# A hybrid decoder step on one core: the input projection from rows laid out turned, with the norm's vector in the weights and the token shift finished by DMA

## The chip, the core and the metric

The kernel runs on one core of a Trainium2 chip: TensorE (PE; its weight loads are shown apart, as PEld), VectorE (DVE), ScalarE (ACT), GpSimd (POOL), and SyncE (SP), which here only issues transfers. The metric is device microseconds for one execution of the whole program, median of several runs. Lower is better.

## What is computed

One inference step of a one-layer decoder over 1024 prompt rows and 64 sample rows (8 sequences of 8), which share all weights. The program is a chain of stages with a barrier between them: projection, mixers (retention and RWKV-7), attention over memory tokens, routing, experts, combination. The change touches the first two:

```python
P = rmsnorm(x, g_mix) @ w_in                  # 1024 -> 3328 columns
ret_p, rw_p = P[..., :1536], P[..., 1536:]    # retention | RWKV
prev = concatenate([s_shift[:, None, :], rw_p[:, :-1]], axis=1)
rw_s = rw_p + (prev - rw_p) * rwkv_mu         # token shift, 1792 columns
s_shift_new = rw_p[:, -1]                     # an output
r, kr, vr, hw, ha, hg = split(rw_s, ...)      # into the RWKV recurrence
```

For the prompt the row before the first is zero; for a sample sequence it is its row of `state_shift`.

## The kernel before

Rows stand in nine tiles of 128: tiles 0 to 7 are the prompt, tile 8 (`NT`) holds the 64 sample rows and 64 rows of padding. Every f32 product is made of three fp32r products: x_hi·w_hi + x_hi·w_lo + x_lo·w_hi, where `hi` is a rounded copy made by ACT and `lo` the remainder made by DVE.

`phase_project` runs over 8 chunks of 416 columns (`NCH`, `W`), and in each over the 9 tiles. Per tile PE makes 8 (`KC`) x 3 matmuls of 128x416: 24 x 9 x 8 = 1728. Ahead of a tile's first use its rows are loaded (`pj_x`), ACT squares and scales them by 1/rms (`norm`, L238 and L240), POOL takes the power (L232), PE turns them (`turn`, L286, 8 transposes), and DVE multiplies by `g_mix` and splits them (L214 to L216). The weights are split a chunk at a time (ACT L254, DVE L199). ACT copies a finished bank out (L247) and stores it to the DRAM array `proj` (L249), one row further down, so that row 0 can be the zero row. PE runs chunks 1 to 6 in a loop of instructions.

`phase_mixers` loads tile j of `proj` (`mx_pin`, 13 KB a row), the RWKV columns of the row above (`mx_prev`) and the rotary table (`mx_rope`), in `load(j)` on SP. DVE does the token shift, three operations over three column ranges: `shift_v` (768 columns), `shift_k` and `shift_r` (512 each), all at L467 to L469. In `pair(i)` these are set between the steps of tile i's triangular inverse: `level(i, l)` is five rounds in which PE makes products with `TTT`, DVE masks them into `X` (L571), PE multiplies again, and ACT copies `TTT` (L854). Tile i+1's preparation is interleaved with it on every engine: POOL's rotation into `mx_qk` (L718 to L723), which PE turns between levels 1 and 2 (L962), ACT's `lora_act` (L783 to L785), which waits for `shift_v`. `load(i + 2)` waits for `r_shifted` of the tile before and for the end of tile i's outputs. The order on each engine is that of the code.

Of the kernel before, what the change touches and what calls it, by code (L numbers as in the profile page):

```python
# [141 lines left out]
def phase_project(core, PS):  # L142
# [8 lines left out]
    NCH = 8  # L151
    W = NIN // NCH
    BUFS = 3
    assert W * NCH == NIN and TILES % BUFS == 0 and W <= 512
    F32R = mybir.dt.float32r
    with ExitStack() as ctx:
        sb = lambda n, s, t=F32: ctx.enter_context(nc.sbuf_tensor("pj_" + n, s, t))
        w, w_hi, w_lo = sb("w", [P, 2, KC, W]), sb("w_hi", [P, 2, KC, W], F32R), sb("w_lo", [P, 2, KC, W], F32R)
        xT, x_hi, x_lo = sb("xT", [P, KC, P]), sb("x_hi", [P, TILES, KC, P], F32R), sb("x_lo", [P, TILES, KC, P], F32R)
        x, sq = sb("x", [P, 2, D]), sb("sq", [P, D])  # L160
        g, ident, expo, st = sb("g", [P, KC]), sb("ident", [P, P]), sb("expo", [P, 1]), sb("st", [P, TILES, 4])
        out = sb("out", [P, BUFS, W])
        as_f32 = lambda ap: ap.bitcast(F32)

        with nc.Block() as block:
            @block.sync
            def _(sp):
                wv = d["w_in"][0].rearrange("(c p) n -> p c n", p=P)

                def load_x(t):  # L170
                    sp.dma_start(x[:, t % 2], d["x"][t * P:(t + 1) * P, :]).then_inc(S_(f"x_loaded{t % 2}"), 16)

                def load_w(c, par):
                    sp.dma_start(w[:, par], wv[:, :, bass.ds(c * W, W)]).then_inc(S_(f"w_loaded{par}"), 16)

                load_x(0)
                sp.dma_start(ident[:], d["ident"][:]).then_inc(S_("consts"), 16)
                with nc.allow_non_contiguous_dma(reason="a gain by channel"):
                    sp.dma_start(g[:], d["g_mix"][0].rearrange("(c p) -> p c", p=P)).then_inc(S_("consts"), 16)
                load_w(0, 0)  # L180
# [11 lines left out]
                sp.wait_ge(S_("zero_stored"), 16)

            @block.vector
            def _(v):
                def split_w(c, par):

                    v.wait_ge(S_("w_high"), c + 1)
                    v.tensor_tensor(w_lo[:, par], w[:, par], as_f32(w_hi[:, par]), ALU.subtract).then_inc(S_("w_split"), 1)  # L199

                def mean_square(t):
                    v.wait_ge(S_("squares"), t + 1)
                    v.tensor_scalar(st[:, t, 1:2], st[:, t, 0:1], 1.0 / D, EPS, ALU.mult, ALU.add).then_inc(S_("ms"), 1)

                lk = Steps(v, S_("dve_first"))
                v.wait_ge(S_("consts"), 32)
                mean_square(0)
                split_w(0, 0)
                mean_square(1)
                for t in range(TILES):  # L210
                    v.wait_ge(S_("turned"), t + 1)
                    src = PS[:, 2 * (t % 2):2 * (t % 2) + 2, :].rearrange("p a (c t) -> p (a c) t", t=P)
                    gain = g[:].unsqueeze(2).to_broadcast([P, KC, P])
                    v.tensor_tensor(xT[:], src, gain, ALU.mult)  # L214
                    lk(v.tensor_tensor(x_hi[:, t], src, gain, ALU.mult))
                    lk(v.tensor_tensor(x_lo[:, t], xT[:], as_f32(x_hi[:, t]), ALU.subtract))  # L216
                    v.sem_inc(S_("xT"), 1)  # L217
                    if t + 2 < TILES:
                        mean_square(t + 2)
                    if t == 4:  # L220
                        split_w(1, 1)
                with v.Fori(0, NCH // 2 - 1) as m:
                    for par in range(2):
                        split_w(2 * m + 2 + par, par)

            @block.gpsimd
            def _(po):
                po.memset(expo[:], -0.5).then_inc(S_("expo"), 1)
                po.wait_ge(S_("expo"), 1)
                for t in range(TILES):  # L230
                    po.wait_ge(S_("ms"), t + 1)
                    po.tensor_tensor(st[:, t, 2:3], st[:, t, 1:2], expo[:], ALU.pow).then_inc(S_("rstd"), 1)  # L232

            @block.scalar
            def _(act):
                def norm(t):
                    act.wait_ge(S_(f"x_loaded{t % 2}"), 16 * (t // 2) + 16)
                    act.activation(sq[:], x[:, t % 2], ACT.Square, accum_out=st[:, t, 0:1]).then_inc(S_("squares"), 1)  # L238
                    act.wait_ge(S_("rstd"), t + 1)
                    act.activation(x[:, t % 2], x[:, t % 2], ACT.Copy, scale=st[:, t, 2:3]).then_inc(S_("xn"), 1)  # L240

                def store(c, t):

                    b = t % BUFS
                    act.wait_ge(S_("projected"), TILES * c + t + 1)
                    act.wait_ge(S_(f"stored{b}"), 16 * (TILES // BUFS * c + t // BUFS) + 16)
                    act.copy(out[:, b], PS[:, 4 + b, 0:W]).then_inc(S_("banked"), 1)  # L247
                    act.wait_ge(S_("banked"), TILES * c + t + BUFS + 1)
                    act.dma_start(d["proj"][t * P + 1:t * P + 1 + P, bass.ds(c * W, W)], out[:, b]).then_inc(S_(f"stored{b}"), 16)  # L249

                def split_w(n, par):

                    act.wait_ge(S_(f"w_loaded{par}"), 16 * n + 16)
                    act.copy(w_hi[:, par], w[:, par]).then_inc(S_("w_high"), 1)  # L254

                for b in range(BUFS):
                    act.sem_inc(S_(f"stored{b}"), 16)
                act.sem_inc(S_("banked"), BUFS)
                norm(0)
                split_w(0, 0)  # L260
                norm(1)
                for t in range(TILES):
                    if t + 2 < TILES:
                        norm(t + 2)
                    store(0, t)
                    if t == 3:
                        split_w(0, 1)
                with act.Fori(0, NCH // 2 - 1) as m:
                    for par in (1, 0):
                        for t in range(TILES):  # L270
                            store(2 * m + 2 - par, t)
                            if t == 3:
                                split_w(m + 1, 1 - par)
                for t in range(TILES):
                    store(NCH - 1, t)
                for b in range(BUFS):
                    act.wait_ge(S_(f"stored{b}"), 16 * (TILES // BUFS * NCH) + 16)

            @block.tensor
            def _(pe):  # L280
                def turn(t):
                    pe.wait_ge(S_("xn"), t + 1)
                    if t >= 2:
                        pe.wait_ge(S_("xT"), t - 1)
                    for c in range(KC):
                        ins = pe.transpose(PS[:, 2 * (t % 2) + c // 4, c % 4 * P:(c % 4 + 1) * P], x[:, t % 2, c * P:(c + 1) * P], ident[:])  # L286
                    ins.then_inc(S_("turned"), 1)

                def project(c, par, t):
                    pe.wait_ge(S_("w_split"), c + 1)  # L290
                    pe.wait_ge(S_("banked"), TILES * c + t + 1)
                    pairs = [(x_hi, w_hi), (x_hi, w_lo), (x_lo, w_hi)]
                    for k in range(KC):
                        for n, (a, b) in enumerate(pairs):
                            ins = pe.matmul(PS[:, 4 + t % BUFS, 0:W], a[:, t, k, :], b[:, par, k, :],  # L295
                                            start=k == 0 and n == 0, stop=k == KC - 1 and n == len(pairs) - 1)
                    ins.then_inc(S_("projected"), 1)
# [2359 lines left out]
```

## Time and profile before

| | us |
|---|---|
| median of 3 runs (lowest to highest) | 2185.8 (2183.77 to 2188.48) |
| the profiled execution, own time | 2183.41 |
| its span, first to last instruction | 2181.6 |
| projection, to the mixers' first instruction | 365.0 |
| mixers, to the attention's first instruction | 519.9 |
| everything behind | 1296.7 |
| PE busy over the span | 1847.1 (85%) |
| DVE busy over the span | 1217.1 (56%) |

The profile is one execution, its times are from the span's start. The shares are averages over stages with different limits, so a change is read in the stage that it touches: which wait ends last there. The barriers between stages let a stage that ends earlier move everything behind it.

### The profile page before, as it was taken

The page shows a single profiled execution, that of the slowest core. Times are in us where ns is not written, and L with a number is a line of the kernel's source. Part 1 is how long each engine was busy: PE and PEld are TensorE (multiplying, and loading weights), DVE is VectorE, ACT ScalarE, POOL GpSimd, SP SyncE. Part 2 cuts the span into 40 slices and gives each one's busy share as a digit, 9 for nine tenths or more (in the row PEclk, how much of TensorE's full clock was granted, in tenths as well). Part 3 has the DMA queues.
Part 4 walks back from the last instruction along what each step waited for, and adds up shares of the span by engine and source line. Part 5 has one row for each costly group of instructions (what it writes and reads, how often), then busy time and mean ns, then how long its engine had stood idle before and what let it go on. Part 6 is the DMA issues. An engine that isn't in the chain of part 4 may idle for free. (4 is left out here: it accounts for less than half of the span.)

```text
span 2181.6 us, 36329 instructions
## 1 busy us (share of the span) xinstructions
PE 1847.1 (85%) x15218; PEld 1559.4 (71%) x15218; DVE 1217.1 (56%) x1285; ACT 835.4 (38%) x923; POOL 305.9 (14%) x262
## 2 busy tenths in 40 slices
PE   5999996687788879589999999854999999999940
PEld 5999996566666667478788888333888888888830
DVE  5200100776788876542333332127899999999926
ACT  4211210332333331340221212003777777777723
POOL 1000000322333323100000000001111111111003
PEclk9999998897999998799999999876999999999975
DMA  4422213417311120855201113526999999999928
GB/s 159 145 79 79 79 49 134 125 60 185 98 65 70 70 62 14 287 213 197 102 29 51 39 59 152 196 85 234 371 404 402 404 403 402 403 402 403 356 102 308
DMA packets 110630, 407.76 MB, mean 187 GB/s; under 512 B 25176, under 2 KB 47960, under 8 KB 82352
## 3 DMA queue, kind: packets, MB, share of 16 engines
q1 hardware_dynamic: 86000, 344.32, 42.6%
q10 hardware_dynamic: 17440, 36.00, 4.4%
q0 software_dynamic: 7072, 25.69, 3.0%
q8 instruction: 96, 1.57, 0.3%
q14 instruction: 22, 0.18, 0.0%
HBM read 345.91 MB, written 68.53 MB: 190 GB/s over the span
## 5 line engine op out<-in xcount | busy, mean ns | idle before, releaser
L2361 DVE TENSOR_TENSOR ex_w_lo<-moe_raw,ex_w_hi 128x2048 fp32r<-128x2048 f32 x192 | 431.2, 2285 | 67.0 <-ACT ex_w_hi L2426 66.9
L2426 ACT CAST ex_w_hi<-moe_raw 128x2048 fp32r<-128x2048 f32 x192 | 364.1, 1913 | 133.3 <-PE banks L2271 90.3
L2271 PE MATMUL banks<-ex_w_hi,ex_x_hi 128*128 128x512 f32 x512 | 208.0, 406 | 10.9 <-issue 6.4
L295 PE MATMUL banks<-pj_w_hi,pj_x_lo 128*128 128x416 f32 x576 | 203.7, 354 | 0.0
L295 PE MATMUL banks<-pj_w_hi,pj_x_hi 128*128 128x416 f32 x576 | 203.3, 353 | 0.1
L2271 PE MATMUL banks<-ex_w_hi,ex_x_lo 128*128 128x512 f32 x512 | 202.1, 395 | 0.0
L2271 PE MATMUL banks<-ex_w_lo,ex_x_hi 128*128 128x512 f32 x512 | 201.5, 394 | 0.0
L295 PE MATMUL banks<-pj_w_lo,pj_x_hi 128*128 128x416 f32 x576 | 201.5, 350 | 0.0
L199 DVE TENSOR_TENSOR pj_w_lo<-pj_w,pj_w_hi 128x3328 fp32r<-128x3328 f32 x8 | 29.0, 3623 | 221.6 <-ACT pj_w_hi L254 221.6
L247 ACT COPY pj_out<-banks 128x416 f32<-128x416 f32 x72 | 36.4, 506 | 253.7 <-PE banks L295 253.7
L2271 PEld LDWEIGHTS banks<-ex_w_hi,ex_x_hi 128*128 128x128 f32 x512 | 97.5, 190 | 42.9 <-issue 21.9
L2271 PEld LDWEIGHTS banks<-ex_w_hi,ex_x_lo 128*128 128x128 f32 x512 | 97.4, 190 | 21.2
L2271 PEld LDWEIGHTS banks<-ex_w_lo,ex_x_hi 128*128 128x128 f32 x512 | 97.7, 191 | 18.6
L295 PEld LDWEIGHTS banks<-pj_w_lo,pj_x_hi 128*128 128x128 f32 x576 | 108.8, 189 | 1.8
L295 PEld LDWEIGHTS banks<-pj_w_hi,pj_x_hi 128*128 128x128 f32 x576 | 108.6, 189 | 1.3 <-DVEq L217 0.7
L295 PEld LDWEIGHTS banks<-pj_w_hi,pj_x_lo 128*128 128x128 f32 x576 | 108.3, 188 | 0.7
L2271 PE MATMUL banks<-ex_w_hi,ex_h_hi 128*128 128x512 f32 x256 | 101.8, 398 | 6.0 <-DVE ex_h_lo L2373 6.0
L2271 PE MATMUL banks<-ex_w_hi,ex_h_lo 128*128 128x512 f32 x256 | 101.8, 398 | 0.0
L2271 PE MATMUL banks<-ex_w_lo,ex_h_hi 128*128 128x512 f32 x256 | 101.6, 397 | 0.0
L2243 POOL COPY ex_idx<-moe_slot_tok 128x1 int32 (+1 forms) x32 | 27.2, 851 | 460.5 <-PE banks L2186 414.3
L957 PE MATMUL banks<-mx_TTT,mx_X 64*64 64x64 f32 x1344 | 79.3, 227 | 14.1 <-DVE mx_X L571 9.6
L1447 POOL TENSOR_TENSOR at_st<-at_st,at_expo 128x1 f32<-128x1 f32 x18 | 9.8, 542 | 542.4 <-DVE at_st L1483 542.4
(375 smaller groups left out, 3823.4 us busy)
## 6 DMA issues: line engine op xcount, KB each, us to landing
moe_raw<-w_e_gate SPq DMA_DIRECT2D x64, 1024.0 KB, 7.7
moe_raw<-w_e_up SPq DMA_DIRECT2D x64, 1024.0 KB, 7.4
moe_raw<-w_e_down SPq DMA_DIRECT2D x64, 1024.0 KB, 7.4
blocks<-ex_y ACTq DMA_DIRECT2D x32, 512.0 KB, 7.7
proj<-pj_out ACTq DMA_DIRECT2D x72, 208.0 KB, 1.9
pj_w<-w_in SPq DMA_DIRECT2D x8, 1664.0 KB, 8.7
mx_pin<-proj SPq DMA_DIRECT2D x8, 1664.0 KB, 7.0
h<-at_h SPq DMA_DIRECT2D x18, 512.0 KB, 2.6
```

Of the source, the lines that this page charges most:

```text
L199: v.tensor_tensor(w_lo[:, par], w[:, par], as_f32(w_hi[:, par]), ALU.subtract).then_inc(S_("w_split"), 1)
L247: act.copy(out[:, b], PS[:, 4 + b, 0:W]).then_inc(S_("banked"), 1)
L295: ins = pe.matmul(PS[:, 4 + t % BUFS, 0:W], a[:, t, k, :], b[:, par, k, :], start=k == 0 and n == 0, stop=k == KC - 1 and n == len(pairs) - 1)
L957: return pe.matmul(out, a, b, start=start, stop=stop, skip_group_check=True)
L1447: po.tensor_tensor(rstd_c(par), ms_c(par), expo[:, 0:1], ALU.pow).then_inc(S_(kind + "_rstd"), 1)
L2243: po.tensor_copy(idx[:, bf:bf + 1], slot_tok[:, bass.ds(n, 1)]).then_inc(S_("idx"), 1)
L2271: ins = pe.matmul(out, a, b, start=first and i == 0, stop=final and i == 2)
L2361: v.tensor_tensor(w_lo[:, j], raw[:, j], as_f32(w_hi[:, j]), ALU.subtract).then_inc(S_("w_split"), 1)
L2426: act.copy(w_hi[:, j], raw[:, j]).then_inc(S_("w_high"), 1)
```

## The change

**Projection.** The host also gives x turned (`xT`, a tile is 4 KB in one piece for each partition), and `w_in` by chunk in one piece for each partition. The chunks are one of 256 columns (3072 to 3327, the low-rank columns) and six of 512: chunks 1 to 3 the retention's, chunks 4 to 6 and chunk 0 are `shifted`. `g_mix` is multiplied into the weights as they are split; 1/rms is multiplied in at eviction. The turns on PE go. Tile 8's stationary operand holds the hi halves of the 64 sample rows in its first 64 columns and the lo halves in the other 64, so two products for each k do (16 matmuls in place of 24), and rows 64 to 127 of the bank are added to rows 0 to 63 (`tmp`). 8 PSUM banks are used in place of 3. For shifted chunks DVE makes p·mu (`pm`) and p − p·mu (`out`) from the bank; SP moves `pm` down one partition by a transfer in SBUF (`up`; 127 rows, and the last row of the tile before apart), POOL adds `up` to `out`, and SP stores. For the sample, eight rows of `up` come from `mu_shift`, state_shift·mu, made once. All stores are on SP now; the two shift states are stored from `raw` here.

**Mixers.** `prev`, `mu`, the three shifts and their waits go; `keys(j)` and `lora_act(j)` wait for the load alone, and `load(j)` no longer waits for `r_shifted`.

```diff
@@ phase_project @@
+    CHUNKS = [(NRET + 3 * WW, NRW - 3 * WW)] + [(512 * c, 512) for c in range(6)]
+    shifted = lambda c: CHUNKS[c][0] >= NRET
 # sync
+                def load_x(t):
+                    if t >= 2:
+                        sp.wait_ge(S_("squares"), t - 1)
...
+                def move_up(c, t):
...
+                    sp.wait_ge(S_("dve_evicted"), dve_evicted(c, t))
+                    if m >= BUFS:
+                        sp.wait_ge(S_("added"), m - BUFS + 1)
+                    sp.dma_start(up[1:r, b, 0:n], pm[0:r - 1, b, 0:n]).then_inc(to, 16)
+                    if t == 0:
+                        sp.dma_start(up[0:1, b, 0:n], d["zero_row"][:, 0:n]).then_inc(to, 16)
+                    elif t < NT:
+                        sp.dma_start(up[0:1, b, 0:n], pm[P - 1:P, (m - 1) % BUFS, 0:n]).then_inc(to, 16)
+                    else:
+                        sp.wait_ge(to, 32 * (m // BUFS) + 16)
...
+                        sp.dma_start(up[0:NS:DS, b, 0:n], d["mu_shift"][:, cols]).then_inc(to, 16)
...
+                for t in range(5, TILES):
+                    load_x(t - 3)
+                    load_xT(t)
+                for t in range(TILES - 3, TILES):
                     load_x(t)
...
+                for c in range(NCH):
+                    if 1 <= c < NCH - 1:
+                        load_w(c + 1, 0)
+                        load_w(c + 1, 1)
+                    for t in range(TILES):
+                        if shifted(c):
+                            move_up(c, t)
+                        if last:
+                            store(*last)
+                        last = (c, t)
+                store(*last)
 # vector
+                def shares(c, t, src, cols):
...
+                    lk(v.scalar_tensor_tensor(pm[0:r, b, 0:width], src, rstd, mu[0:r, cols], ALU.mult, ALU.mult))
...
+                    out_free(v, c, t)
+                    v.scalar_tensor_tensor(out[0:r, n % BUFS, 0:width], src, rstd, pm[0:r, b, 0:width], ALU.mult, ALU.subtract).then_inc(S_("dve_evicted"), 1)
 # gpsimd
+                        po.wait_ge(S_("dve_evicted"), dve_evicted(c, t))
+                        po.wait_ge(S_(f"up{m % BUFS}"), 32 * (m // BUFS + 1))
+                        po.tensor_tensor(o, o, up[0:r, m % BUFS, 0:width], ALU.add).then_inc(S_("added"), 1)
 # tensor
+                        if n >= 8:
+                            b, u = divmod(n - 8, TILES)
+                            if shifted(b) or u == NT:
+                                pe.wait_ge(S_("dve_evicted"), dve_evicted(b, u))
...
+                        terms = [(x_hi, w_hi), (x_hi, w_lo), (x_lo, w_hi)][0:3 if t < NT else 2]
@@ phase_mixers @@
                 def load(j):
                     if j >= 1:
-                        sp.wait_ge(S_("r_shifted"), j)
                         sp.wait_ge(S_("qk_ready"), j)
...
-                        sp.dma_start(prev[r], d["proj"][j * P:j * P + n, OR:NIN]).then_inc(to, 16)
...
                     level(i, 1)
-                    shift_v(j)
+                    keys(j)
                     level(i, 2)
-                    shift_k(j)
-                    keys(j)
+                    key_sum(j)
                     level(i, 3)
                     ret_sum(i)
                     turned_lora(j)
-                    key_sum(j)
                     level(i, 4)
                     rates(j)
                     if i >= 1:
                         y_sum(i - 1)
-                    shift_r(j)
                     level(i, 5)
...
                 def lora_act(j):
-                    act.wait_ge(S_("v_shifted"), j + 1)
+                    act.wait_ge(S_(f"loaded{j % 2}"), loads_of(j))
```

How it stands on the engines. First VectorE in the mixers, levels 1 to 3 of a prompt tile (`mx_X` is a level's masked product, `mx_prev` the row above, `mx_kk` the keys). Before:

```order
L571 TENSOR_TENSOR mx_X<-banks,mx_lev 128x256 x2
L467 TENSOR_TENSOR mx_prev<-mx_prev,mx_pin 128x768
L468 TENSOR_TENSOR mx_prev<-mx_prev,mx_mu 128x768
L469 TENSOR_TENSOR mx_pin<-mx_pin,mx_prev 128x768
L571 TENSOR_TENSOR mx_X<-banks,mx_lev 128x256 x2
L467 TENSOR_TENSOR mx_prev<-mx_prev,mx_pin 128x512
L468 TENSOR_TENSOR mx_prev<-mx_prev,mx_mu 128x512
L469 TENSOR_TENSOR mx_pin<-mx_pin,mx_prev 128x512
L482 TENSOR_TENSOR mx_kk<-mx_pin,mx_vec 128x512
L571 TENSOR_TENSOR mx_X<-banks,mx_lev 128x256 x2
```

and now:

```order
L700 TENSOR_TENSOR mx_X<-banks,mx_lev 128x256 x2
L612 TENSOR_TENSOR mx_kk<-mx_pin,mx_vec 128x512
L700 TENSOR_TENSOR mx_X<-banks,mx_lev 128x256 x2
L616 TENSOR_REDUCE mx_stk<-mx_t 128x8
L617 TENSOR_SCALAR mx_stk<-mx_stk 128x8
L700 TENSOR_TENSOR mx_X<-banks,mx_lev 128x256 x2
```

Six shift operations are gone from between the levels (three more from ahead of level 5), and the keys' sum has moved up. Second SyncE in the projection, from the last rows loaded to the first tiles of chunk 0; before there was no counterpart (the stores were ACT's). Now:

```order
L203 DMA pj_xT<-xT 128x1024
L208 DMA pj_x<-x 128x1024
L203 DMA pj_xT<-xT 128x1024
L208 DMA pj_x<-x 128x1024
L203 DMA pj_xT<-xT 128x1024
L208 DMA pj_x<-x 128x1024 x3
L259 DMA mu_shift<-pj_ss 128x112
L217 DMA pj_up<-pj_pm 127x256
L219 DMA pj_up<-zero_row 1x256
L217 DMA pj_up<-pj_pm 127x256
L221 DMA pj_up<-pj_pm 1x16x16
L240 DMA proj<-pj_out 128x256
```

The first move (L217) stands behind the last load of x, which waits for the squares of tile 6. Third SyncE at the projection's end, tiles 7 and 8 of chunk 6, where ACT's queue held one store a tile before:

```order
L217 DMA pj_up<-pj_pm 127x512
L221 DMA pj_up<-pj_pm 1x16x32
L228 DMA out_shift_p<-pj_raw 1x512
L240 DMA proj<-pj_out 128x512
L217 DMA pj_up<-pj_pm 63x512
L226 DMA pj_up<-mu_shift 8x512
L230 DMA out_shift_s<-pj_raw 8x512
L240 DMA proj<-pj_out 128x512
L240 DMA proj<-pj_out 64x512
```

Tile 8's last store stands behind two moves that follow one another (L217, L226); the store ahead of it is tile 7's.

## Rows read from the trace of the kernel before

**Rows 1.** Stretches: start:end, length, PE, PEld, DVE, ACT, POOL busy (count), PE clock, DMA share, GB/s.

```profile
0.00:20.95 20.95, 3.71 (x16) 3.14 (x16) 7.33 (x6) 9.78 (x10) 1.38 (x7) 1.00 0.70 241
20.95:361.45 340.50, 335.49 (x1785) 330.99 (x1784) 54.44 (x38) 71.55 (x97) 7.10 (x7) 0.99 0.24 84
364.98:409.80 44.82, 16.16 (x98) 10.44 (x99) 22.23 (x36) 8.31 (x17) 10.14 (x12) 0.60 0.90 275
655.00:703.50 48.50, 38.76 (x916) 32.87 (x916) 40.97 (x66) 17.67 (x34) 18.24 (x14) 0.96 0.20 73
752.40:807.80 55.40, 42.15 (x916) 35.94 (x920) 40.83 (x66) 17.72 (x34) 16.90 (x14) 0.88 0.28 66
```

**Rows 2.** Groups of instructions from 0 to 361.45 us.

```profile
L286 PE MATMUL banks<-pj_ident,pj_x 128*128 128x128 f32 x72 | 12.0, 323 | 22.2 <-ACT pj_x L240 22.2
```

**Rows 3.** Timeline, the first projection's start and its end.

```profile
20.95 0.71 PE L295 MATMUL banks<-pj_w_hi,pj_x_hi 128*128 128x416 f32 x1
...
361.49 0.51 ACT L247 COPY pj_out<-banks 128x416 f32<-128x416 f32 x1 [4.03 <-PE banks L295]
364.98 0.35 SPq L400 DMA_DIRECT2D mx_pin<-proj  x1
```

**Rows 4.** The page's slices: GB/s moved.

```profile
GB/s 159 145 79 79 79 49 134 125 60 185 98 65 70 70 62 14 287 213 197 102 29 51 39 59 152 196 85 234 371 404 402 404 403 402 403 402 403 356 102 308
```

**Rows 5.** Timeline of PE in the attention stage.

```profile
1129.78 0.39 PE L1777 MATMUL banks<-at_y_lo,at_a_hi 128*128 128x512 f32 x1
1133.86 0.39 PE L1777 MATMUL banks<-at_y_lo,at_a_hi 128*128 128x512 f32 x1
1141.00 1.87 PE L1874 MATMUL banks<-at_wr,at_qT 128*128 128x36 f32 x16
1149.64 0.39 PE L1777 MATMUL banks<-at_x_lo,at_o_hi 128*128 128x512 f32 x1
1154.77 0.39 PE L1778 MATMUL banks<-at_x_hi,at_o_lo 128*128 128x512 f32 x1
```

**Rows 6.** Timeline, the mixers' start.

```profile
371.19 2.28 ACTq L904 DMA_DIRECT2D mx_chunk<-chunk_s  x1
383.76 0.96 DVE L467 TENSOR_TENSOR mx_prev<-mx_prev,mx_pin 128x768 f32<-128x768 f32 x1 [18.10 <-DMA mx_g<-rwkv_g]
389.40 0.28 DVE L495 COPY mx_loT<-banks 128x128 f32<-128x128 f32 x1
```

**Rows 7.** Timeline of one mixer tile: POOL, PE, DVE.

```profile
680.30 0.73 POOL L718 TENSOR_TENSOR mx_qk<-mx_pin,mx_rope 128x256 f32<-128x256 f32 x1 [5.74 <-DMA mx_rope<-rope]
...
686.78 0.66 PE L962 MATMUL banks<-mx_ident,mx_qk 128*128 128x128 f32 x4 [1.23 <-POOL mx_qk L723]
701.29 1.15 PE L957 MATMUL banks<-mx_TTT,mx_X 64*64 64x64 f32 x32 [1.04 <-DVE mx_X L571]
...
665.72 1.75 DVE L530 TENSOR_TENSOR mx_stage<-mx_pin,mx_ex 128x512 f32<-128x512 f32 x1
688.90 0.68 DVE L467 TENSOR_TENSOR mx_prev<-mx_prev,mx_pin 128x512 f32<-128x512 f32 x1
691.69 0.89 DVE L571 TENSOR_TENSOR mx_X<-banks,mx_lev 128x256 f32<-128x256 f32 x2
700.82 0.75 DVE L571 TENSOR_TENSOR mx_X<-banks,mx_lev 128x256 f32<-128x256 f32 x2
```

**Rows 8.** Waits from 752 to 808 us (total, times, longest).

```profile
POOL mx_qk L718 <- DMA mx_rope<-rope: 12.2, 1, 12.2
PE banks L962 <- POOL mx_qk L723: 4.5, 1, 4.5
DVE mx_prev L467 <- DMA mx_prev<-state_shift: 4.0, 1, 4.0
```

**Rows 9.** DMA issues, 0 to 800 us: KB each, median us to landing.

```profile
proj<-pj_out ACTq DMA_DIRECT2D x72, 208.0 KB, 1.9
mx_rope<-rope SPq DMA_DIRECT2D x8, 256.0 KB, 9.3
```

More of the change, by code:

```diff
@@ new lines, in store @@
+                def store(c, t):
+                    n, (col, width) = number(c, t), CHUNKS[c]
+                    if shifted(c):
+                        sp.wait_ge(S_("added"), moved(c, t) + 1)
+                    elif t < NT:
+                        sp.wait_ge(S_("act_evicted"), act_evicted(c, t))
+                    else:
+                        sp.wait_ge(S_("dve_evicted"), dve_evicted(c, t))
+                    sp.dma_start(d["proj"][t * P:t * P + rows_of(t), col:col + width], out[0:rows_of(t), n % BUFS, 0:width]).then_inc(S_(f"stored{n % BUFS}"), 16)
@@ L176, in _ @@
+                load_w(0, 0)
+                load_xT(0)
+                load_w(0, 1)
+                load_xT(1)
+                load_xT(2)
                 load_x(0)
[L177 to L180, printed above, removed]
+                load_w(1, 0)
@@ L192, in _ @@
[L192 removed]
+                sp.wait_ge(S_("shift_ready"), 1)
+                sp.dma_start(d["mu_shift"].rearrange("b n -> (b n)").rearrange("(p n) -> p n", p=P), ss[:]).then_inc(S_("shift_stored"), 16)
+                last = None
+                for c in range(NCH):
[3 more added lines that the diff above has]
+                    for t in range(TILES):
+                        if shifted(c):
+                            move_up(c, t)
+                        if last:
+                            store(*last)
+                        last = (c, t)
@@ L201, in mean_square @@
[L201 to L221, printed above, removed]
@@ new lines, in evict @@
+                def evict(c, t):
+                    n, (col, width) = number(c, t), CHUNKS[c]
+                    cols = slice(col - NRET, col - NRET + width)
+                    v.wait_ge(S_("projected"), n + 1)
+                    v.wait_ge(S_("rstd"), t + 1)
+                    src = PS[:, n % 8, 0:width]
+                    if t < NT:
+                        shares(c, t, src, cols)
+                    else:
+                        v.wait_ge(S_("tmp"), c + 1)
+                        lk(v.tensor_tensor(tmp[:, 0:width], src[0:NS], tmp[:, 0:width], ALU.add))
+                        if shifted(c):
+                            shares(c, t, tmp[:, 0:width], cols)
+                        else:
+                            out_free(v, c, t)
+                            v.tensor_scalar(out[0:NS, n % BUFS, 0:width], tmp[:, 0:width], st[0:NS, t, 2:3], None, ALU.mult).then_inc(S_("dve_evicted"), 1)
@@ new lines, in _ @@
+                v.wait_ge(S_("g_loaded"), 16)
+                for k in range(HALF):
+                    w_low(0, k)
+                x_low(0)
+                for k in range(HALF, KC):
+                    w_low(0, k)
+                for t in range(1, 4):
+                    x_low(t)
+                v.wait_ge(S_("mu_loaded"), 48)
+                v.tensor_tensor(ss[:], ss[:], mus[:], ALU.mult).then_inc(S_("shift_ready"), 1)
+                x_low(4)
+                evict(0, 0)
+                x_low(5)
@@ new lines, in _ @@
+                evict(0, 1)
+                x_low(6)
+                evict(0, 2)
+                x_low(7)
+                for k in range(HALF):
+                    w_low(1, k)
+                x_low(8)
+                for k in range(HALF, KC):
+                    w_low(1, k)
+                for t in range(3, TILES):
+                    evict(0, t)
+                for c in range(1, NCH):
+                    for t in range(TILES):
+                        if shifted(c) or t == NT:
+                            evict(c, t)
+                        if c + 1 < NCH and t < KC:
+                            w_low(c + 1, t)
@@ L230, in _ @@
                 for t in range(TILES):
+                    po.wait_ge(S_("squares"), t + 1)
+                    po.tensor_scalar(st[:, t, 1:2], st[:, t, 0:1], 1.0 / D, EPS, ALU.mult, ALU.add).then_inc(S_("ms"), 1)
                     po.wait_ge(S_("ms"), t + 1)
                     po.tensor_tensor(st[:, t, 2:3], st[:, t, 1:2], expo[:], ALU.pow).then_inc(S_("rstd"), 1)
+                for c in range(NCH):
+                    if not shifted(c):
+                        continue
+                    for t in range(TILES):
+                        m, r, width = moved(c, t), rows_of(t), CHUNKS[c][1]
+                        o = out[0:r, number(c, t) % BUFS, 0:width]
+                        po.wait_ge(S_("dve_evicted"), dve_evicted(c, t))
+                        po.wait_ge(S_(f"up{m % BUFS}"), 32 * (m // BUFS + 1))
+                        po.tensor_tensor(o, o, up[0:r, m % BUFS, 0:width], ALU.add).then_inc(S_("added"), 1)
@@ L234, in _ @@
             @block.scalar
             def _(act):
[L236 to L277, printed above, removed]
+                def w_high(c, k):
+                    n, i = CHUNKS[c][1], 2 * c + k // HALF
+                    act.wait_ge(S_(f"w_loaded{i % 3}"), 16 * (i // 3 + 1))
+                    if c >= 2:
+                        act.wait_ge(S_("projected"), TILES * (c - 1))
+                    src = piece(c, k // HALF)[:, k % HALF * n:(k % HALF + 1) * n]
+                    act.activation(w_hi[:, c % 2, k, 0:n], src, ACT.Copy, scale=g[:, k:k + 1]).then_inc(S_("w_high"), 1)
@@ new lines, in x_high, with square, evict @@
+                def x_high(t):
+                    act.wait_ge(S_(f"xT_loaded{t % 3}"), 16 * (t // 3 + 1))
+                    act.copy(x_hi[:, t, :, 0:rows_of(t)], xT[:, t % 3, :, 0:rows_of(t)]).then_inc(S_("x_high"), 1)
+                def square(t):
+                    act.wait_ge(S_(f"x_loaded{t % 2}"), 16 * (t // 2 + 1))
+                    act.activation(x[:, t % 2], x[:, t % 2], ACT.Square, accum_out=st[:, t, 0:1]).then_inc(S_("squares"), 1)
+                def evict(c, t):
+                    n, width = number(c, t), CHUNKS[c][1]
+                    act.wait_ge(S_("projected"), n + 1)
+                    if t == NT:
+                        if c >= 1:
+                            act.wait_ge(S_("dve_evicted"), dve_evicted(c - 1, NT))
+                        act.copy(tmp[:, 0:width], PS[NS:P, n % 8, 0:width]).then_inc(S_("tmp"), 1)
+                    else:
+                        act.wait_ge(S_("rstd"), t + 1)
+                        out_free(act, c, t)
+                        act.activation(out[:, n % BUFS, 0:width], PS[:, n % 8, 0:width], ACT.Copy, scale=st[:, t, 2:3]).then_inc(S_("act_evicted"), 1)
@@ new lines, in _ @@
+                x_high(1)
+                x_high(2)
+                square(0)
+                x_high(3)
+                square(1)
+                x_high(4)
+                x_high(5)
+                square(2)
+                x_high(6)
+                square(3)
+                x_high(7)
+                for k in range(HALF):
+                    w_high(1, k)
+                x_high(8)
+                for k in range(HALF, KC):
+                    w_high(1, k)
+                for t in range(4, TILES):
+                    square(t)
@@ L279, in _ @@
+                evict(0, NT)
+                for c in range(1, NCH):
+                    for t in range(TILES):
+                        if not shifted(c) or t == NT:
+                            evict(c, t)
+                        if c + 1 < NCH and t < KC:
+                            w_high(c + 1, t)
             @block.tensor
             def _(pe):
[L281 to L297, printed above, removed]
@@ L644, in _ @@
                 key_sum(0)
-                shift_r(0)
                 rates(0)
```

189 lines of the change are left out of this document (118 added, 71 removed).

## The prediction

> **What bounds the kernel now.** I read the stretches first, to see which engine is full where the change touches [rows 1]. From 20.95 to 361.45 us PE is busy 335.5 of 340.5 us at a granted clock of 0.99, DVE 54, ACT 72: the projection is PE's. Its head, 0 to 20.95, is a chain of load, square, scale, turn and split with PE busy 3.7 us. The mixers' head (364.98 to 409.8) runs at a DMA share of 0.90. A prompt tile of the mixers (655 to 703.5) takes 48.5 us with DVE busy 41.0 and PE 38.8, so neither is full and the dependences decide; there I read the timeline. The last prompt tile takes 55.4. Everything behind the mixers is untouched and, with barriers between the stages, only moves.
>
> **The projection: PE.** Before, 1728 matmuls of 416 columns; PE's 340.5 us contain them and 56 of the 72 turns, of which the group takes 12.0 us busy [rows 2]. Now a chunk is 8 x 24 + 16 = 208 matmuls: 208 of 256 columns and 1248 of 512. The attention stage has fp32r matmuls of 512 columns back to back: 18 steps from 1129.78 to 1133.86 (0.227 us each), and 22 steps from 1149.64 to 1154.77 (0.233) [rows 5]. I take 0.230: 1248 x 0.230 = 287 us, with 283 and 291 as its bounds. For 256 columns no row has this form. From below, weight load and matmul of 36 columns go 16 in 1.87 us, 0.117 each [rows 5]; from above, 416 columns cost 340.5 / 1728 = 0.197 with all between them [rows 1]. Columns alone scale 0.230 to about 0.12, next to the lower end: 208 x 0.12 = 25 us (bounds 24 and 41).
>
> The Trainium skill (TensorE: Matmul & The Clock Gate, Back-to-back issue gap) gives 518 cycles for an isolated matmul of 512 columns, 0.216 us. By that the six chunks would be 269 us and the sum 18 us lower. The rows say 0.227 to 0.233, and the rows decide.
>
> **The projection: start.** The first matmul waits for half of chunk 0's weights (512 KB), a turned tile, four small splits on ACT, a copy and a DVE subtraction; before, the squares, the power and a turn stood in it too and it began at 20.95 [rows 3]. I put it at 10. What then counts is when chunk 1 starts. Three clocks run: PE needs 10 + 25 = 35. The transfers up to the ninth turned tile are 3.1 MB of weights, 4.7 of xT, 3.1 of x and 1.0 of mu and shift state, 12 MB: 30 us at the 402 GB/s of the page's full slices [rows 4], or 43 at the 275 of the mixers' head [rows 1]; with the splits behind them 34 or 47. DVE's splits and first evictions until then are about 33 times 512 columns, at 0.68 [rows 7] 22 us, and ACT's work is as much, interleaved. I take 36, and bounds of 35 and 60 (PE at half clock through chunk 0: 10 + 50).
>
> SP issues chunk 0's first move behind the last load of x, which waits for ACT's squares of tile 6, done near 40. DVE's fourth eviction waits for it, for POOL's add and a store, some 48 us; PE wants that bank at chunk 1's third tile, 36 + 11 = 47. I allow a stall of 2 us. Beyond that, moves, adds and stores for a 512-column tile must fit 24 x 0.230 = 5.5 us, and with 8 banks PE is eight tiles clear. So PE ends at 36 + 287 + 2 = 325, against 361.45: 36 less.
>
> **The projection: end.** Before, from the last bank (361.45) to the mixers' first instruction was 3.5 us: a copy of 0.5, a store, the barrier [rows 3]. Now the sample's last bank goes through ACT's copy (0.6), four DVE operations (0.68 each, the time of one on 128x512 [rows 7]), the move and then the mu_shift rows, each an issue of 0.35 and a landing of 1.9 [rows 3, 9], POOL's add (about 1.3), and the same store and barrier (3.0): 0.6 + 2.7 + 4.5 + 1.3 + 3.0 = 12, so 9 more (bounds 5, if the moves overlap with DVE, and 13 at landings of 4). **The projection stage: 36 − 9 = 27 us less.**
>
> **The mixers' head.** DVE's first shift starts at 383.76, when the first constants have landed, and the low-rank transpose is copied at 389.40 [rows 6]. Gone are 0.9 MB of mu and 0.9 MB of prev: at 275 GB/s [rows 1] 6.5 us, at 402 4.5. Gone too are 5 us of shifts between the two times. But ACT issues eighteen transfers before it can do `lora_act`, up to 2.3 us each [rows 6], and the later constants still have to land. Of 10 us I take 6.5 (bounds 3 and 10).
>
> **A prompt tile.** Removed from DVE: three operations of 0.96 and six of 0.68, 7.0 us [rows 6, 7]. Three places:
> - Levels 1 to 2. PE waits 1.23 us for POOL's rotation [rows 7], which waited for the load (5.74). The load lands a median 9.3 us after the issue of its last part [rows 9] and shrinks from 2.8 to 1.9 MB, so POOL starts some 2.5 us earlier and PE's wait goes: 1.2 gained. `shift_v` itself hid behind PE.
> - Levels 2 to 3. DVE turns to X at 691.69, as it is free and as PE's product is there [rows 7]: 0.1.
> - Levels 4 to 5. X starts at 700.82, late by `shift_r`; PE sat idle 1.04 before 701.29 [rows 7]: 1.1.
>
> Against it: POOL now rotates while DVE makes the mask and the first X, on the path. A DVE operation beside POOL took 1.75 where one alone took 0.68 [rows 7]; one half of such a hit is 0.5. So 2.4 − 0.5 = about 2 a tile, and 16 us for eight (bounds 0 and 7.0 a tile).
>
> The Trainium skill (SBUF — State Buffer, Who interferes with whom) says that a DVE instruction with two SBUF inputs and a GpSimd instruction that reads SBUF lock each other out. That rule speaks against this change twice: at the mask's followers here, and in the projection, where POOL's new adds meet DVE's weight splits. The two durations of rows 7 agree with it. In the projection by it a split costs 1.3 more, 8 a chunk: 10 us, under a PE that has 47 us a chunk.
>
> **The last prompt tile.** It takes 55.4 us against 48.5 [rows 1]: POOL waited 12.2 us for the halved loads, PE 4.5 for POOL, DVE 4.0 for the shift states' rows [rows 8]. Four transfers are left of six and the shift rows are gone. I take 5 (bounds 0 and 6.9).
>
> **Sum.** 27 + 6.5 + 16 + 5 = 54.5 us. The profiled execution took 2183.4, so 2128.9; the median of the runs is 2.4 above it: **2131**.
>
> **The rivals.**
> - *Cold or starved start.* After its waits PE is granted less (0.60 in the mixers' head [rows 1]); if chunk 0's tiles come in too thinly, it runs at 1.2 GHz, or the loads run at 275 GB/s. Chunk 1 then starts at 48 to 60 rather than 36: 12 to 24 back, 2150. Against it: once started, tiles follow every 3 us.
> - *The tiles do not move.* The gains at PE are taken back by POOL's collisions with DVE's masks: 16 back, 2147.
> - *The whole shift comes off.* DVE is busiest in a tile, 41.0 of 48.5; if its order is the true bound, 7.0 a tile come off in place of 2: 40 more, 2091. Against it: the rows of the tile show PE waiting for 2.3 us in all [rows 7].
> - *Slower: SP's queue becomes the projection's bound.* A shifted tile needs three transfers issued in order, each behind waits, and two in a chain through POOL. With issues of 2.3 us, as the mixers' head shows them on a full queue [rows 6], that is 6.9 us a tile against PE's 5.5; 27 tiles of 512 columns give back 37 us. It turns the sum over at 5.5 + 54.5 / 27 = 7.5 us a tile, and at 6.9 + 1.9 = 8.8, with a landing [rows 9] in the chain as well, it gives 2131 + 27 x 3.3 = 2220. Against it: issues in a quiet queue take 0.35 [rows 3], and weights are the only other traffic.
>
> **How the numbers follow.** My forecast (2112 to 2145 in its own right): 0.58. Cold or starved start: 0.15. Tiles unmoved: 0.11. Whole shift: 0.12. SP's queue: 0.04. The first three lie between 2109 and 2158; the lower bounds together (3 us a tile, 10 at the head, matmuls at 0.227, an end of 5, no stall) give 2131 − 8 − 3.5 − 4 − 4 − 2 = 2109, and I go part of the way from there to the whole shift. So 2100 to 2158, which leaves out that rival and SP's. A measurement of this kernel tells 0.2% (4 us) from no change. Only the slower rival lies above: slower 0.04, within 0.2% 0.01, faster 0.95.
>
> **What would show it.** Right: first matmul near 10 us, chunk 1 from 36, steps of 0.23 us with PE idle under 3 us to the end near 325, about 12 us to the mixers' first instruction; a tile period near 46.5 with no PE wait on `mx_qk` and none on level 5's X; the last prompt tile near 48. Wrong: PE waiting in chunks 4 to 6 on DVE's evictions; a first chunk at clock 0.5; `mx_M` and `mx_X` at 1.3 us and more in every tile; or a stage behind the mixers that changes its length, which I do not expect.

## The result, and the profile after

The changed kernel takes 2297.55 us (median of 4, 2296.56 to 2300.45) where the kernel before, on the same chip, takes 2187.14: a ratio of 1.051, 95% interval 1.049 to 1.053. It is 5% slower; 2131 had been forecast. The profiled execution has a span of 2294.8, 113.2 more than before.

The stages, in us, from the first instruction of each. The last column is all behind the mixers, which before end at 885.05.

| kernel | projection | mixers | rest |
|---|---|---|---|
| before | 365.0 | 520.1 | 1296.6 |
| after | 496.3 | 502.1 | 1296.4 |
| forecast | 338 | 492.6 | unchanged |

So the loss is the projection's, 131.3 us; the mixers gain 18.0. The stretches of the changed kernel, columns as in [rows 1]:

```profile
0.00:35.00 35.00, 22.52 (x168) 22.12 (x168) 15.47 (x23) 18.11 (x27) 3.25 (x13) 1.00 0.88 344
35.00:100.00 65.00, 54.29 (x247) 44.75 (x248) 13.73 (x25) 11.19 (x20) 10.73 (x19) 0.92 0.21 67
100.00:206.00 106.00, 101.55 (x431) 82.68 (x430) 21.49 (x30) 31.77 (x50) 0.00 (x0) 0.95 0.35 130
206.00:302.00 96.00, 72.47 (x299) 58.33 (x298) 23.13 (x31) 5.71 (x9) 10.26 (x8) 0.84 0.14 53
302.00:399.00 97.00, 54.17 (x213) 42.21 (x212) 21.63 (x29) 5.71 (x9) 11.50 (x9) 0.74 0.19 68
399.00:495.00 96.00, 23.88 (x106) 19.45 (x104) 14.81 (x19) 0.58 (x1) 12.68 (x10) 0.65 0.14 51
```

The third retention chunk runs at PE's pace of 5.44 us a tile and ends at 203.6, where the forecast has 182; what came in between is taken up under *moves* below. Each shifted chunk of 512 columns takes 96 to 97 us, 10.7 a tile in place of 5.5. PE starts it with free banks, but in the last one it is busy for 24 of 96 us, DVE 15 and POOL 13, and the transfers move 51 GB/s. When nothing is busy, ask what everything waits for. The waits of the same kernel from 206 to 495 us (sum, times, longest):

```profile
POOL pj_out L378 <- DMA pj_up<-pj_pm: 199.8, 21, 9.6
DVE pj_pm L304 <- DMA pj_up<-pj_pm: 170.1, 20, 9.3
...
PE banks L465 <- DVE pj_w_lo L289: 66.4, 8, 10.0
```

All lead to the move of `pj_pm` into `pj_up`: POOL's add and DVE's next share wait for it, DVE's weight split is queued behind DVE's share, and PE waits for the split, so its granted clock falls too. SP's timeline, L217 the move of 127 rows, L221 the one-row move, L240 a store, and POOL's adds (L378), each of which starts as a move lands:

```profile
226.67 0.65 SPq L217 DMA_DIRECT2D pj_up<-pj_pm  x1
227.37 9.17 SPq L221 DMA_DIRECT2D pj_up<-pj_pm  x1
236.58 0.58 SPq L240 DMA_DIRECT2D proj<-pj_out  x1
237.26 0.65 SPq L217 DMA_DIRECT2D pj_up<-pj_pm  x1
237.96 9.80 SPq L221 DMA_DIRECT2D pj_up<-pj_pm  x1
...
234.66 1.29 POOL L378 TENSOR_TENSOR pj_out<-pj_out,pj_up 128x512 f32<-128x512 f32 x1 [9.28 <-DMA pj_up<-pj_pm]
245.45 1.29 POOL L378 TENSOR_TENSOR pj_out<-pj_out,pj_up 128x512 f32<-128x512 f32 x1 [9.50 <-DMA pj_up<-pj_pm]
```

The adds follow tile by tile, and the one at 245.45 is that of the move issued at 226.67: from issue to landing it took 18.8 us. So two moves are in flight at a time, and one lands every 10.8 us. The issue of 2 KB takes 9 us: it ends at 236.5, 1.9 after the move of the tile before has landed. The slices of 226 to 236 us, a quarter microsecond each:

```profile
DMA  0010688310000000000000000000000030000000
GB/s 25 25 32 25 246 344 320 131 66 33 25 25 25 25 25 33 25 25 25 25 25 25 25 33 25 25 25 25 25 25 25 25 90 33 25 25 25 25 25 25
```

and two microseconds with nothing but a move, with the columns of [rows 1]:

```profile
232.00:234.00 2.00, 2.00 (x10) 1.69 (x9) 0.00 (x0) 0.00 (x0) 0.00 (x0) 1.00 0.06 25
```

The store passes at up to 344 GB/s in about a microsecond. The move goes on at 25 GB/s with a share of 0.06 of the 16 DMA engines, and one of sixteen is 0.0625. Its 127 rows of 2 KB at 25 GB/s are 10.4 us, near the 10.8 between two landings. So one engine of the sixteen does it.

That was the first theory: **127 rows, a prime, are not dealt out over the engines.** The Trainium skill (DMA: Bandwidth & Descriptors, Why a DMA increments its semaphore by 16 and not by 1) gives the rule: a transfer uses the largest number of engines up to 16 that divides its slowest dimension, 1 for 127. The share of 0.06 agrees. Rivals: transfers from SBUF to SBUF are slow however they are dealt out; or it is SP's queue, my fourth rival, with its issues and waits, and the move is only where the queue is seen to stand.

### The profile page after: what moved, and what is told of

The parts are those of the page before. It is cut to its first block and busy times, and to the rows that moved or that the text cites. A ratio compares the mean times of both kernels' runs of the same rounds, so it can differ in the third digit from the quotient of the medians.

```text
span 2294.8 us, 35637 instructions
## 1 busy us (share of the span) xinstructions
PE 1835.5 (80%) x14874; PEld 1493.4 (65%) x14874; DVE 1201.1 (52%) x1316; ACT 825.8 (36%) x930; POOL 342.3 (15%) x307
## 5 line engine op out<-in xcount | busy, mean ns | idle before, releaser
L465 PE MATMUL banks<-pj_w_hi,pj_x_hi 128*128 128x512 f32 (+1 forms) x504 | 197.3, 392 | 94.0 <-DVE pj_w_lo L289 70.8
L2394 PE MATMUL banks<-ex_w_hi,ex_x_hi 128*128 128x512 f32 x512 | 208.0, 406 | 10.8 <-issue 6.3
L465 PE MATMUL banks<-pj_w_lo,pj_x_hi 128*128 128x512 f32 (+1 forms) x504 | 194.6, 387 | 0.0
L465 PEld LDWEIGHTS banks<-pj_w_hi,pj_x_hi 128*128 128x128 f32 x504 | 98.8, 196 | 119.7 <-DVE pj_w_lo L289 74.2
L465 PE MATMUL banks<-pj_w_hi,pj_x_lo 128*128 128x512 f32 (+1 forms) x448 | 173.3, 387 | 0.0
L304 DVE SCALAR_TENSOR_TENSOR pj_pm<-banks,pj_st,pj_mu 128x512 f32<-128x512 f32 (+1 forms) x32 | 21.9, 683 | 221.7 <-DMA pj_up<-pj_pm 185.8
L465 PEld LDWEIGHTS banks<-pj_w_lo,pj_x_hi 128*128 128x128 f32 x504 | 99.4, 197 | 16.9
L378 POOL TENSOR_TENSOR pj_out<-pj_out,pj_up 128x512 f32<-128x512 f32 (+3 forms) x36 | 41.1, 1140 | 400.4 <-DMA pj_up<-pj_pm 234.6
L465 PEld LDWEIGHTS banks<-pj_w_hi,pj_x_lo 128*128 128x128 f32 x448 | 88.6, 198 | 16.3
L289 DVE SCALAR_TENSOR_TENSOR pj_w_lo<-pj_w,pj_g,pj_w_hi 128x512 fp32r<-128x512 f32 (+1 forms) x56 | 38.7, 709 | 102.2 <-ACT pj_w_hi L388 102.2
```

The lines of the kernel that those rows point to most:

```text
L289: v.scalar_tensor_tensor(w_lo[:, c % 2, k, 0:n], src, g[:, k:k + 1], as_f32(w_hi[:, c % 2, k, 0:n]), ALU.mult, ALU.subtract).then_inc(S_(" ...
L304: lk(v.scalar_tensor_tensor(pm[0:r, b, 0:width], src, rstd, mu[0:r, cols], ALU.mult, ALU.mult))
L378: po.tensor_tensor(o, o, up[0:r, m % BUFS, 0:width], ALU.add).then_inc(S_("added"), 1)
L465: ins = pe.matmul(PS[:, n % 8, 0:width], xs[:, t, k, :], ws[:, c % 2, k, 0:width], start=k == 0 and a == 0, stop=k == KC - 1 and a == len( ...
L2394: ins = pe.matmul(out, a, b, start=first and i == 0, stop=final and i == 2)
```

## The experiments on the move

**The move cut in two.** The sums that the waits compare with grow from 32 to 48 a use.

```diff
-sp.dma_start(up[1:r, b, 0:n], pm[0:r - 1, b, 0:n]).then_inc(to, 16)
+cut = 112 if t < NT else 48
+sp.dma_start(up[1:cut + 1, b, 0:n], pm[0:cut, b, 0:n]).then_inc(to, 16)
+sp.dma_start(up[cut + 1:r, b, 0:n], pm[cut:r - 1, b, 0:n]).then_inc(to, 16)
```

> The move of 127 rows is cut into 112 and 15, the sample's 63 rows into 48 and 15; one more transfer a tile on SP's queue, the same bytes. Theory (the move goes through one DMA engine, since 127 rows are not dealt out): 112 rows are dealt to 16 engines and 15 to 15, so a move lands in about 2 us in place of 9 to 10, the tile period in the shifted chunks falls from 10.9 to PE's 5.5, the projection stage ends at 335 to 345 in place of 496, and the kernel takes 2135 to 2150 us. Rival (a transfer from SBUF to SBUF is slow however it is dealt out): landing stays near 9 us, 2290 to 2300. Rival (SP's queue is full of issues and waits, and the move is only where the queue is seen to stand): a third transfer makes a tile longer by an issue of 0.35 to 2.3 us, 2300 to 2360.

Two controls are the same kernel but for the cut, `113` and `122` in place of `112`:

> As the kernel with 112 and 15 rows, with one row moved from one part to the other: 113 and 14 (the sample's part the same, 48 and 15). 113 is prime as 127 is. Theory: 226 KB through one engine at 27 GB/s are 8.4 us, and with the 1.5 us that a tile takes beside the move now the period is 9.9 in place of 10.9: 27 tiles, 27 us less and a little from the first chunk, the kernel 2260 to 2275. Rivals of either kind: the same time as with 112 and 15 rows, whatever that is.

> As before, cut at 122 (2 x 61) and 5. Theory, as the slowest dimension is dealt out in equal shares over a number of engines that divides it: 122 goes to 2 engines, 244 KB at 2 x 27 GB/s is 4.5 us, and with 1.5 beside it the tile period is 6.0: PE's 5.5 is just missed, the projection stage ends at 350 to 375, and the kernel takes 2150 to 2180. If rows are dealt out without regard to divisors and 127 is slow for another reason, it equals one of the two others.

| rows | rows of the first part | us (lowest to highest, 4 runs) | ratio to before (95%) | projection |
|---|---|---|---|---|
| 112 + 15 | 16 x 7 | 2143.57 (2140.97 to 2150.19) | 0.981 (0.979 to 0.983) | 340.4 |
| 122 + 5 | 2 x 61 | 2163.07 (2158.58 to 2165.71) | 0.989 (0.987 to 0.990) | 357.9 |
| 113 + 14 | prime | 2269.93 (2267.75 to 2274.63) | 1.038 (1.037 to 1.040) | 467.6 |
| 127 | prime | 2297.55 | 1.051 | 496.3 |

All three times fall where the theory put them; with 122 + 5 a tile took 5.6 us and not 6.0. One row shifted from a part to the other, with the same bytes and the same count of transfers, is worth 126 us, and both rivals forecast no difference. SP's timeline with 112 + 15 (L218 and L219 the two parts, L223 the one row, L242 the store):

```profile
213.68 0.53 SPq L218 DMA_DIRECT2D pj_up<-pj_pm  x1
214.25 0.84 SPq L219 DMA_DIRECT2D pj_up<-pj_pm  x1
215.14 0.55 SPq L223 DMA_DIRECT2D pj_up<-pj_pm  x1
215.73 1.76 SPq L242 DMA_DIRECT2D proj<-pj_out  x1
219.12 0.53 SPq L218 DMA_DIRECT2D pj_up<-pj_pm  x1
```

its issues (KB each, median us to landing) and its stretches:

```profile
pj_up<-pj_pm SPq DMA_DIRECT2D x24, 224.0 KB, 2.5
```

```profile
206.00:326.50 120.50, 120.31 (x531) 99.29 (x529) 49.93 (x66) 6.45 (x11) 29.95 (x23) 1.00 0.34 113
326.50:340.40 13.90, 0.00 (x0) 0.00 (x0) 3.45 (x4) 0.43 (x1) 2.57 (x3) 0.62 0.23 73
```

A tile each 5.44 us, PE's own pace, with four issues of 0.5 to 1.8 in it; PE is full to 326.5. With 113 + 14 the second issue takes 7 us instead of 0.8:

```profile
231.96 0.65 SPq L218 DMA_DIRECT2D pj_up<-pj_pm  x1
232.65 7.03 SPq L219 DMA_DIRECT2D pj_up<-pj_pm  x1
239.73 0.54 SPq L223 DMA_DIRECT2D pj_up<-pj_pm  x1
240.31 0.58 SPq L242 DMA_DIRECT2D proj<-pj_out  x1
241.00 0.65 SPq L218 DMA_DIRECT2D pj_up<-pj_pm  x1
```

and with 122 + 5 the slices between the stores' peaks (211 to 234 us) are at twice 25, and from 219.5 to 222.5 the share of the engines is 0.14 (two of sixteen are 0.125):

```profile
GB/s 50 53 278 224 50 61 53 50 53 50 50 53 370 132 82 57 53 50 53 50 50 114 378 64 54 60 51 50 53 50 50 178 317 57 64 53 50 50 50 53
```

**Two queues.** The changed kernel with 127 rows; the odd tiles' moves of the last three chunks are issued by ACT, behind its weight split of that tile and the same waits:

```diff
-sp.dma_start(up[1:r, b, 0:n], pm[0:r - 1, b, 0:n]).then_inc(to, 16)
+if not on_act(c, t):   # shifted, c > 0 and t odd
+    sp.dma_start(up[1:r, b, 0:n], pm[0:r - 1, b, 0:n]).then_inc(to, 16)
...
```

> The changed kernel with moves of 127 rows, but in the three shifted chunks of 512 columns those of tiles 1, 3, 5 and 7 are issued by ACT, the others by SP as now. If a move through one engine goes to an engine of its own for each queue (or the engines take turns), two of 9.4 us overlap, a tile takes about 5.5 to 6.5 us and the stage ends at 345 to 385: 2150 to 2190. If such a move always goes to the same engine, whichever queue it comes from, the period stays near 9.5 to 11: 2270 to 2300. A queue that is slow in itself (the rival on SP's queue) would give the first as well, so this tells only what the one engine is, not that there is one.

It took 2298.67 us (ratio 1.051, 1.049 to 1.052): no change. Its timeline:

```profile
228.28 0.66 SPq L221 DMA_DIRECT2D pj_up<-pj_pm  x1
...
237.54 0.63 ACTq L453 DMA_DIRECT2D pj_up<-pj_pm  x1
...
247.81 0.75 DVE L308 SCALAR_TENSOR_TENSOR pj_pm<-banks,pj_st,pj_mu 128x512 f32<-128x512 f32 x1 [9.64 <-DMA pj_up<-pj_pm]
258.00 0.75 DVE L308 SCALAR_TENSOR_TENSOR pj_pm<-banks,pj_st,pj_mu 128x512 f32<-128x512 f32 x1 [7.42 <-DMA pj_up<-pj_pm]
```

and a stretch with two moves in flight and no store:

```profile
239.00:247.00 8.00, 8.00 (x37) 6.64 (x36) 0.00 (x0) 0.61 (x1) 0.00 (x0) 1.00 0.07 26
```

DVE waits until 247.8 for the move issued at 228.3 and until 258.0 for that of 237.5. As before two moves are in flight at a time, now from two queues; each takes 20 us, and from 226.5 to 280.1 one lands every 10.7. Together they move 26 GB/s at a share of 0.07, what one move had alone. So both queues use the same engine: a second queue doesn't mend it. The Trainium skill, in the same section (DMA: Bandwidth & Descriptors, Why a DMA increments its semaphore by 16 and not by 1), says that the lowest-numbered engines are taken; this run agrees as far as it can show.

## The experiment on the mixers' tile

A steady tile did not gain: from 723.49 to 870.32 us the retention's stores of the changed kernel come every 48.9 us, before (606.47 to 752.38) every 48.6. DVE's timeline in one of these tiles:

```profile
752.25 0.89 DVE L700 TENSOR_TENSOR mx_X<-banks,mx_lev 128x256 f32<-128x256 f32 x2
753.06 0.68 DVE L612 TENSOR_TENSOR mx_kk<-mx_pin,mx_vec 128x512 f32<-128x512 f32 x1
756.06 0.89 DVE L700 TENSOR_TENSOR mx_X<-banks,mx_lev 128x256 f32<-128x256 f32 x2 [2.32 <-PE banks L1080]
759.81 0.69 DVE L616 TENSOR_REDUCE mx_stk<-mx_t 128x8 f32<-128x512 f32 x1 [2.86 <-ACT mx_t L922]
760.53 0.17 DVE L617 TENSOR_SCALAR mx_stk<-mx_stk 128x8 f32<-128x8 f32 x1
760.61 0.75 DVE L700 TENSOR_TENSOR mx_X<-banks,mx_lev 128x256 f32<-128x256 f32 x2
```

The `X` of levels 1 to 2 follow in 3.81 us (5.11 in the tile of [rows 7]), but 2 to 3 take 4.55 where [rows 7] have 3.59. The change moved `key_sum` ahead of level 3, and its reduction waits for ACT's square, which ACT makes behind its copies of level 2: a wait in the place of the one removed. DVE spent 29.5 us in nine such waits. The experiment puts it back:

```diff
 level(i, 2)
-key_sum(j)
 level(i, 3)
 ret_sum(i)
 turned_lora(j)
+key_sum(j)
 level(i, 4)
```

> The changed kernel, projection untouched, with DVE's key_sum(j) moved back from before level 3 to behind turned_lora(j), where it stood before the change. Theory (the wait of DVE's mx_stk on ACT's key_square took the place of the removed shifts): level 2 to 3 goes from 4.6 back to about 3.7 us, the tile period falls from 48.4 by 0.9 to 1.5, eight tiles, the kernel 7 to 12 us less: 2286 to 2291. Rival (POOL's rotations, now beside DVE's masks, took back the gain): no change, 2295 to 2300.

2291.70 us (2289.25 to 2295.77), ratio 1.048 (1.047 to 1.050), about 6 less than the changed kernel, 0.7 above the range expected; the two were not timed together, so the edit was tried again on the mended projection:

> Both edits together: moves of 112 and 15 rows, and key_sum(j) back behind turned_lora(j). If the two losses are independent, the sum is the projection stage of the first (ends at 340.4), mixers of 494 to 496 us as with key_sum back alone, and the 1297 of the rest: 2131 to 2136 us, 7 to 10 under the kernel with 112 and 15 rows alone. If the gain of key_sum came only from how the tiles happened to lie after the slow projection, 2143.

2135.80 us (2130.83 to 2139.46), ratio 0.977 (0.975 to 0.978) against 0.981 (0.979 to 0.983): the two losses add. In both traces one wait of 0.2 is left of the nine, level 2 to 3 is back at 3.59 in every steady tile, and the mixers take 494.1 and 493.5 us.

**What is left in a tile.** With `key_sum` back all four steps from level 1 to 5 are 3.81, 3.59, 4.28, 3.86, but the time from `mx_TTT` to the first `X` is 4.2, 4.6 or about 6.2. The same instructions before [of the tile of rows 7] and with `key_sum` back, first DVE, then PE:

```profile
678.78 0.69 DVE L566 TENSOR_TENSOR mx_TTT<-mx_X,mx_i 128x512 f32<-128x512 f32 x1
679.53 0.65 PE L957 MATMUL banks<-mx_TTT,mx_i 64*64 64x256 f32 x4 [1.97 <-DVE mx_TTT L566]
680.01 0.63 PE L957 MATMUL banks<-mx_i,mx_TTT 64*64 64x64 f32 x16
```

```profile
741.97 1.09 DVE L695 TENSOR_TENSOR mx_TTT<-mx_X,mx_i 128x512 f32<-128x512 f32 x1
743.12 1.12 PE L1080 MATMUL banks<-mx_TTT,mx_i 64*64 64x256 f32 x4 [1.62 <-DVE mx_TTT L695]
744.03 1.06 PE L1080 MATMUL banks<-mx_i,mx_TTT 64*64 64x64 f32 x16
```

The second again, as a stretch:

```profile
743.10:746.60 3.50, 3.48 (x42) 2.71 (x44) 3.31 (x5) 0.37 (x1) 3.26 (x5) 0.50 0.02 5
```

Two things: `mx_TTT` took 0.40 more beside POOL's rotation, and PE's four groups ran at a granted clock of 0.50, 1.2 GHz, after its waits, where the first of them took 0.65 before, at 1.00 (2.4 GHz): by the starts 0.9 a group in place of 0.47, 1.7 us for four. The kernel before has a tile with the second as well: from `mx_TTT` at 727.36 to the first `X` at 733.15 are 5.79 us, with a granted clock of 0.62 from 728.1 to 731.5. The next experiment separates them, on the best kernel (below):

```diff
 if j >= 1:
     po.wait_ge(S_("ret_done"), j)
+    po.wait_ge(S_("TT_first"), j)
```

> The kernel with retention last, and POOL's rotation of tile j waits until DVE has made mx_TTT of tile j-1, so that it no longer lies beside it. In the three traces with key_sum back, mx_TTT takes 1.09 us where the rotation lies beside it and 0.69 where not, and the time from mx_TTT to the first X of the levels is 4.2, 4.6 or 6.0 to 6.4. Theory A (the collision of POOL and DVE costs 0.4, and the 6.2 is another thing, PE's products at a granted clock of 0.5 after a wait): mx_TTT is 0.69 in every tile, the values left are 4.2 and about 5.8, and PE waits up to 1 us for mx_qk where the clock is full; in all 0 to 4 us less, which is hardly to be told: 2125 to 2132. Theory B (the collision is also behind the 6.2): every tile is at 4.2, 8 to 12 us less, 2117 to 2121.

`mx_TTT` takes 0.69 in all nine tiles, PE waits once, 0.8, for the rotation in the whole stage, and still two of the steady tiles have 5.95 and 5.66: theory A, with the clock at 0.50 and 0.52 there. The mixers take 490.9 us in this trace and 493.6 in that of the kernel without the wait; the time, 2133.34 us (2127.29 to 2135.09; ratio 0.976, 0.975 to 0.977), can't be told from that kernel's and is 1 above the range expected. What decides in which tile the clock falls stays open.

## The best version

The end of the projection was the last term to try: with retention chunks last, no move stands behind PE's last matmul. The host lays the weights out in the same order, and the three functions that count the evictions count over that order.

```diff
-CHUNKS = [(NRET + 3 * WW, NRW - 3 * WW)] + [(512 * c, 512) for c in range(6)]
+CHUNKS = [(NRET + 3 * WW, NRW - 3 * WW)] + [(512 * c, 512) for c in (3, 4, 5, 0, 1, 2)]
```

> The kernel with both edits, and the chunks in another order: the four shifted ones first and the three of retention last (weights laid out in that order too). Theory: from PE's last matmul (326.4) to the mixers' first instruction (340.4) it now takes 14 us, since the sample's last tile goes through copy, four DVE operations, two transfers in a chain, POOL's add and a store; with a retention chunk last it is a copy, an add, a scale and the store, 5 to 6 us, so 8 to 9 us less: 2122 to 2128. Rival (the early shifted chunks meet the weights' and tiles' loads and the late splits, and PE waits for DVE's evictions in chunk 1 or 2): the gain is lost there, 2130 to 2140.

2128.78 us (2127.04 to 2138.94), ratio 0.9745 (0.9725 to 0.9766) against 0.9768 (0.9752 to 0.9783) on the same chip: 5 us by the ratios and 7 by the medians, and the intervals overlap. The traces tell it more surely: from the start of ACT's last copy (330.32) to the mixers' first instruction (335.70) are 5.4 us where there were 14, and PE's own end came 3 later than in the kernel with both edits, partly since it waits 2.15 at 97.43 for a weight split. Both theories held a part: the median lies 1 above the first one's range.

## Why the prediction was wrong

**Projection, start: right in its first matmul**, at 9.82 (forecast 10); chunk 1 starts at 40.7, 5 later than the 36 forecast, at a full granted clock. Then chunk 0's moves hold PE up: it waits 9.79 us at 61.60, where I had allowed 2, and 4.5 more behind them for late weight splits (103.87 and 107.85). With 112 + 15 the first of these waits is 2.08.

**Projection, moves: wrong, and this is the step.** The text had "the move and then the mu_shift rows, each an issue of 0.35 and a landing of 1.9 [rows 3, 9]", and that moves, adds and stores "must fit 5.5 us", which I then took as given. The row for 1.9 is a store of 128 rows. A move of 127 keeps one engine for over 10 us and lands 18.8 after its issue. It cost 27 x (10.7 − 5.5) = 140 of the 158 us by which the stage missed. Another 22 were lost before the shifted chunks (203.6 for 182), 5 of them at the start and most of the others behind chunk 0's moves; the end, where the 63 rows and the `mu_shift` rows follow each other (480.8 to 491.6), is partly in the 10.7 already, and the forecast's 12 for it were not all added.

**Projection, all else: near, in part by luck.** Mended by one cut, PE ends at 326.5 (forecast 325) and the stage at 340.4 (338), the end taking 13.9 where I had 12. Two misses cancel in the 326.5: chunk 1 started 3 late there (39.2), and matmuls follow every 0.227 us, at my lower bound, which is 4 less over the six chunks.

**The rival "SP's queue" had the right place and the wrong cause.** I priced it at 8.8 us a tile and 2220. The queue stood, but not from its own issues: with one transfer more it keeps 5.44 a tile. Its chance of 0.04 rested on issues and never asked how fast a move is.

**Mixers' head: right in size.** To the first retention store, with the first tile in it, 66.8 us in place of 74.4, 7.6 less (forecast 6.5).

**A steady tile: mis-sized, 2 forecast, about 0 measured.** Three parts. The new wait behind `key_sum` cost 0.97: I had noted the removals and not what was moved past what. The levels themselves gained 1.3 (X1 to X5 of the tiles at 586.95 and 635.40: 16.82, with `key_sum` back 15.54), not 2.4: PE's wait of 1.23 for POOL [rows 7] occurs once in the four tiles from 558 to 752 us, in the one I had read. And 0.40 from POOL (forecast 0.5) and 1.7 from the clock, in some tiles, go against it, though one tile before had the second too. So the rival "the tiles do not move" names what happened here, and its cause, POOL's collisions, is 0.40 of it; the wait behind `key_sum` was in no rival.

**The last prompt tile: right**, 49.0 against 55.4, 6.4 less (5). The first tile of the loop gained as much, 44.8 against 51.3, which I had not counted. That is why, with `key_sum` back, the mixers' sum (26.0 less) came out near the forecast 27.5 by other terms.

With its two losses undone the change takes 2135.80 us, where I had forecast 2131 for it as it stood.

## What to carry to other kernels

Price a transfer by a row with the same shape and route: before counting bytes, factor its row count, since moves of 127 rows in one transfer landed every 10.8 us, 18.8 after their issue, and 112 and 15 rows 2.5 after theirs. Where no row has the shape, let the upper bound be the rate of one engine, here 25 GB/s, and not the landing of a neat transfer. When work is moved, list for each moved wait what its producer has queued ahead of it; and take a tile's waits from several tiles, not from the one on the page.

## What was not expected of the hardware

- One engine moves rows of 2 KB at 25 to 27 GB/s, two at 50 to 53, while a store of 128 rows beside it peaks at 344.
- Behind moves in one engine the next issue on the queue takes 7 to 9.8 us (L221 9.17, L219 7.03), about until the move of the tile before has landed; behind one over two engines 0.74.
- Moves of 127 rows from SP's and ACT's queues share one engine: 20 us each, two at a time, 26 GB/s in all; from SP's queue alone they take 19.
- Of two tiles with the same instructions one has PE's products at a granted clock of 0.50 and one at 1.00, 1.7 us apart. This is so before the change as well.
